# A two-layer decoder trunk: the order of Pool's adding transfers, and of three VectorE steps where the FFN begins

## What is computed

```python
for layer in range(DEPTH):                      # DEPTH = 2
    ...                                         # the mixing part: h = h + mix
    hn = rms_norm(h, norm_ffn_g[layer])
    h = h + (jax.nn.silu(hn @ ffn_w_gate[layer]) * (hn @ ffn_w_up[layer])) @ ffn_w_down[layer]
return rms_norm(h, norm_final_g)
```

## Time and profile before

| | |
|---|---|
| median of 3 runs | 561.09 us (559.78 to 562.26) |
| the profiled execution, its own time | 559.87 us |
| its span, first to last instruction | 558.0 us |
| granted PE clock | 0.999 of full speed, all through |
| PE busy | 548.7 us (98%) |
| DVE busy | 474.1 us (85%) |
| ACT busy | 348.9 us (63%) |

### The profile page before, as it was taken

The page is one execution under the profiler, slowest core; times in us unless marked ns, Lnnn a source line. Parts: engine busy times, 40 slices in busy tenths (PEclk is TensorE's granted clock), DMA queues, the critical chain, the costliest instruction groups (busy, mean ns, idle before and its releaser), DMA issues.

```text
span 558.0 us, 7380 instructions
## 1 busy us (share of the span) xinstructions
PE 548.7 (98%) x2805; PEld 461.0 (83%) x2805; DVE 474.1 (85%) x564; ACT 348.9 (63%) x475; POOL 29.0 (5%) x70
## 2 busy tenths in 40 slices
PE   8999999999999999999999999999999999999996
PEld 7899978887888788888888888888788888878785
DVE  5769996798989999878798998977989898989765
ACT  6877664664767486655666366646576666748524
POOL 1200001100000010000000000001010000000000
PEclk9999999999999999999999999999999999999999
DMA  8995546845979879774469422409789697977102
GB/s 295 409 404 196 189 150 211 270 123 132 298 258 286 307 203 340 189 286 167 151 256 346 174 76 76 151 29 292 284 221 339 187 314 243 295 284 211 56 0 75
DMA packets 32867, 122.42 MB, mean 219 GB/s; under 512 B 3648, under 2 KB 4800, under 8 KB 30784
## 3 DMA queue, kind: packets, MB, share of 16 engines
q1 hardware_dynamic: 30384, 105.04, 49.8%
q0 software_dynamic: 2304, 16.78, 15.7%
q10 hardware_dynamic: 144, 0.14, 0.1%
HBM read 120.89 MB, written 1.05 MB: 219 GB/s over the span
## 4 chain that ended last, share of the span: by engine, by line
PE 71%; DVE 16%; DMA 5%; issue 4%; ACT 3%; POOL 0%; SPq 0%; DVEq 0%; ACTq 0%; POOLq 0%
PE bank L1792 12%; PE bank L1794 12%; PE bank L1793 12%; DVE w_lo L1133 7%; PE bank L2266 5%; PE bank L2265 5%; PE bank L2270 5%; PE bank L1903 4%; PE bank L2237 3%; DMA spare<-in_slabs 2%; DMA sixth_raw<-in_slabs 2%; PE bank L1906 2%; DVE raw L1597 2%; PE bank L2242 1%; ACT w_hi L682 1%
## 5 line engine op out<-in xcount | busy, mean ns | idle before, releaser
L1133 DVE TENSOR_TENSOR w_lo<-raw,w_hi 128x2048 fp32r<-128x2048 f32 (+2 forms) x71 | 156.2, 2211 | 21.5 <-ACT w_hi L682 21.0
L682 ACT ACTIVATE w_hi<-raw 128x2048 fp32r<-128x2048 f32 (+2 forms) x66 | 120.8, 1846 | 5.0 <-DMA raw<-in_slabs 2.8
L1792 PE MATMUL bank<-w_lo,yT_hi 128*128 128x512 f32 (+1 forms) x226 | 91.3, 404 | 2.2 <-DVE yT_lo L1690 1.6
L1794 PE MATMUL bank<-w_hi,yT_lo 128*128 128x512 f32 (+1 forms) x226 | 88.1, 390 | 0.0
L1793 PE MATMUL bank<-w_hi,yT_hi 128*128 128x512 f32 (+1 forms) x226 | 87.8, 389 | 0.0
L1133 DVE TENSOR_TENSOR w_lo<-sixth_raw,w_hi 128x2048 fp32r<-128x2048 f32 x22 | 50.3, 2285 | 5.0 <-ACT w_hi L682 5.0
L1792 PEld LDWEIGHTS bank<-w_lo,yT_hi 128*128 128x128 f32 x226 | 42.5, 188 | 13.1 <-DVE yT_lo L1690 4.2
L2265 PE MATMUL bank<-w_hi,forms_hi 128*128 128x512 f32 x128 | 50.4, 394 | 0.0
L1794 PEld LDWEIGHTS bank<-w_hi,yT_lo 128*128 128x128 f32 x226 | 42.4, 188 | 9.1
L2266 PE MATMUL bank<-w_hi,forms_lo 128*128 128x512 f32 x128 | 49.9, 390 | 0.0
L1793 PEld LDWEIGHTS bank<-w_hi,yT_hi 128*128 128x128 f32 x226 | 42.6, 189 | 7.4
(11 more groups left out here) (289 smaller groups left out, 1136.5 us busy)
## 6 DMA issues: line engine op xcount, KB each, us to landing
raw<-in_slabs SPq DMA_DIRECT2D x146, 512.0 KB, 7.7
sixth_raw<-in_slabs SPq DMA_DIRECT2D x28, 512.0 KB, 7.6
sixth_raw<-in_slabs POOLq DMA_DIRECT2D x6, 1024.0 KB, 11.3
spare<-in_slabs SPq DMA_DIRECT2D x12, 512.0 KB, 4.9
raw<-in_slabs POOLq DMA_DIRECT2D x6, 1024.0 KB, 8.8
spare<-in_slabs POOLq DMA_DIRECT2D x4, 1024.0 KB, 10.4
raw<-in_slabs SPq DMA_DIRECT2D x5, 256.0 KB, 4.6
h<-in_x SPq DMA_DIRECT2D x2, 512.0 KB, 6.7
```

What stands on the lines that cost most here:

```text
L682: A(w_of(s, c), raw_of(r, c), ACT.Copy).then_inc(hi_ready, 1)
L1133: V.tensor_tensor(w_of(s, c, 1), raw_of(preps[s][0], c), w_of(s, c).bitcast(F32), ALU.subtract).then_inc(lo_ready, 1)
L1792: T.matmul(o, st_hi, mv_lo, start=first, stop=False, skip_group_check=onto)
L1794: return T.matmul(o, st_lo, mv_hi, start=False, stop=last, skip_group_check=onto)
```

## The change

There are two edits. First, Pool's order becomes T3(2), T4(2), T3(4), T3(6), T4(4), T3(8), T4(6), T4(8) in each layer. With two T3 possibly under way, `third_added` becomes two semaphores used in turn. Second, in the FFN's entry the gate `activate(3, 1)` and the low part `at_lo_evac(2, 0, 0, 1)` come ahead of the split of slab `f + 6`.

```diff
-        third_added = sem("third_added")
+        third_added = [sem(f"third_added{i}") for i in range(2)]
...
+        def third_sum(l, a):
+
+            n = seven_no(l, a)
+            return third_added[n % 2], 16 * (n // 2) + 16
+
         sum_of_prep = {}
...
-                sum_of_prep[place["t3", l, a]] = (third_added, 16 * seven_no(l, a) + 16)
+                sum_of_prep[place["t3", l, a]] = third_sum(l, a)
...
-                nc.gpsimd.dma_start(raw_of(y), piece(n, 0, SLAB), accum_op=ALU.add).then_inc(third_added, 16)
+                nc.gpsimd.dma_start(raw_of(y), piece(n, 0, SLAB), accum_op=ALU.add)\
+                    .then_inc(third_sum(l, a)[0], 16)
...
                 if (kind, a, b) in (("norm", 1, 1), ("norm", 3, 1)):
-                    for unit in SEVEN_AT[a // 2]:
-                        add_third(a // 2, unit)
-                        add_fourth(a // 2, unit)
+                    l, units = a // 2, SEVEN_AT[a // 2]
+                    add_third(l, units[0])
+                    add_fourth(l, units[0])
+                    add_third(l, units[1])
+                    for unit, following in zip(units[1:], units[2:]):
+                        add_third(l, following)
+                        add_fourth(l, unit)
+                    add_fourth(l, units[-1])
...
-                        dve.wait_ge(third_added, 16 * seven_no(l, a) + 16)
+                        dve.wait_ge(*third_sum(l, a))
...
                 block_add(SEVEN_AT[l][0], 0)
-                split_los(f + 6)
                 activate(3, 1)
                 at_lo_evac(2, 0, 0, 1)
+                split_los(f + 6)
                 split_forms()
```

## The result

| | before | after |
|---|---|---|
| median | 560.59 us (559.78 to 562.26) | 571.44 us (570.99 to 572.99) |
| ratio | | 1.0195, 95% interval 1.0163 to 1.0226 |
| profiled execution, own time | 559.87 us | 572.99 us |
| its span | 558.0 us | 571.2 us |

The change makes the kernel about 2% slower. The forecast was 571.0, and the time lies in its range of 562 to 577.

What follows compares the result with a forecast made beforehand. PE was taken as the bound, busy 548.7 of 558.0 us. 559.87 + 6.0 (layer 0) + 6.0 (layer 1) - 1.4 = 570.5; that execution lies 1.2 under the median, so 571, range 562 to 577.

Steps and rivals of the forecast that it cites:

- Pool's hold: Pool's queue: an adding transfer starts only 0.3 us after the one before has landed, so T4(4) waits for T3(6).
- The transfers: Unit 4's transfers to landing: T3(6) takes 9.0 us, T4(4) in the crowd 11.1, with bounds 7.8 twice and 12.6 twice.
- ACT's copy at landing + 4.2: ACT, unit 4: seven_copy(4, 2), needed by PE for b22, ends 4.2 us after T4(4) lands; layer 0 loss 5.7.
- DVE's way at landing + 14.0: DVE behind T4(4): PE's restart at 189.35 moves to landing plus 14.0, 195.4, 6.0 us later; the longer way.
- Layer 0: Unit 4 of layer 0: T4(4) lands at 181.4 instead of 174.6, costing +6.0 us, entry gain included.
- Layer 1: Unit 4 of layer 1: T4(4) lands at 456.4, the copy ends at 460.6 against b22 at 454.67, costing +6.0 us.
- The break in unit 8: Layer 1, block_add(8, 0): the wait for T3(8) goes, and with it PE's break at 495.89, -1.4 us.
- The entry: FFN entry: low part ready before PE needs it, worth 0.6 us in each layer unless lost at the next late thing.
- Quick transfers: Rival: T3(6) and T4(4) take 7.8 us each, sum 561.5, no change; chance 0.08.
- slow ones: Rival: T3(6) and T4(4) take 12.6 us each, +11.1 in each layer, sum 580.7; slow end beyond 577 has 0.06.
- Pool doesn't hold T4: Rival: T4(4) starts at 165.1 behind T3(6) and lands about as before; all four breaks go, 556.7 us; chance 0.08.
- the four breaks: PE's breaks in the FFNs, by the entry in both layers, at 189.35 and at 495.89: together 3.2 us, the most to gain.

Runs made afterwards that it cites:

- the run with 34 idle matmuls: Changed kernel with idle matmuls ahead of PE's wait at b22 of unit 4, 28 in layer 0 and 34 in layer 1: 571.33 us, ratio 1.0216.
- the run with twice the room: Changed kernel with descriptor room 1024 for 512 and five small buffers moved to make space: 562.38 us, ratio 1.0054.
- the aligned run: Changed kernel with room 1024, nmax and sums placed behind spare so forms_hi and forms_lo start at a multiple of 128 bytes: 561.17 us, ratio 1.0031.
- T4 first and room for both: Kernel before, with its Pool order kept, plus the entry edit and room 1024 with forms at a multiple of 128 bytes: 556.68 us, ratio 0.9950.

## Why the prediction was right, and where not

**Pool's hold.** Right: T4(4) starts 0.31 after T3(6) has landed, in both layers. That it is the same for a T4 behind a T3 was read from six T3 behind T4, and it held. The cause, which the prediction didn't have, is the descriptor room.

**The transfers.** T3(6) was put at 9.0 and took 7.9 and 8.1; T4(4) was put at 11.1 and took 12.7 and 10.8. The choice which of the two is quiet and which is in the crowd was right, and the sum of 20.1 stands against 20.6 and 18.9. In layer 0 the two errors offset each other (1.1 too high and 1.6 too low); in layer 1 both terms were too high. T4(4) of layer 0 went 0.1 past the upper bound of 12.6.

**The ways behind the landing.** ACT's copy at landing + 4.2 is exact (186.60, from 182.38). DVE's way at landing + 14.0 is nearly so: its low part ended at 196.52, which is 14.1. But the conclusion, that DVE's way is the longer one and sets +6.0, was wrong. PE reached the matmul that reads this low part only at 197.69, 1.2 after DVE was done:

```profile
196.10 0.42 DVE L1701 TENSOR_TENSOR yT_lo<-bank,yT_hi 128x256 fp32r<-128x256 f32 x1
...
197.69 0.39 PE L1803 MATMUL bank<-w_lo,yT_hi 128*128 128x512 f32 x1
```

The step that failed is that PE was taken to keep the pace of the earlier trace rows behind the break. At that pace PE would have come to this matmul 8.9 us behind b22, at 195.6, before DVE was done. With the clock at the lower level for 4 us, PE itself was the later one. The slow stretch costs 1.5 to 1.6 us in each layer between b22 and b11, as the run with 34 idle matmuls showed; 1.2 of it stands beyond DVE's way in layer 0.

**The terms.** Layer 0 was put at +6.0 and is +8.2: the landing is 1.0 later than forecast (182.4 for 181.4), and PE is another 1.2 behind DVE's way. Layer 1 was put at +6.0 and is +6.4, counted from the end of layer 0 (7.1 less the 0.7 that the entry gave). That it is so near is luck: counted in the same way the landing came 1.2 earlier than forecast (455.2 for 456.4) and b22 is +4.8, and the slow stretch, which was not in the sum, adds 1.6. The prediction also took ACT's way here and DVE's in layer 0, without a reason for the difference. The break in unit 8 was put at -1.4 and is -1.4. T4(6) was said not to be held, and is not. The sum of 570.5 for the profiled execution stands against 572.99 measured. So that 571 stands beside a median of 571.44 is in part luck, and closer than the terms are: the profiled execution was the slowest of its four, and the other three took 571.0 to 571.6.

**The entry.** Right in what it does (no break at 126, and none in layer 1) and in what it warned of, that it is lost again at the next late thing. In the changed kernel that is T4(4), in the kernel before the low parts behind a late T3. It wins about 1.5 once neither is late, which is near the 0.6 in each layer that the prediction put on it.

**The rivals.** Quick transfers (561.5) and slow ones (580.7) did not come. (The quick case lay outside the range of 562 to 577, though the prediction counted most of it in.) "Pool doesn't hold T4" was ruled out here, and the run with twice the room made its condition true: it gave 562.4, and 561.2 with the aligned layout, not 556.7. Its price took T4(4)'s landing as unchanged, and a transfer that moved beside another of its kind landed later (176.8 in the aligned run, 174.6 before). What it got right is the worth of the four breaks, 3.2: with T4 first and room for both they went, and the time was 556.68, 2.9 under the kernel before beside it. And the six T3 showed that Pool held a transfer with the room of 512; they did not show that it can't have two under way.

**Not settled.** Why 571.0 and 576.5 can both be times of the changed kernel stays open. The longest execution with a trace took 572.99; the one of 576.5 has none, and of it is known only that its granted clock was lower (0.979 over the whole, 0.987 to 0.988 in the other three of that set). How long T4(4) takes in the crowd was not controlled in any run.

## What to carry to other kernels

An idle time that the profile puts down to "issue" can have a holder that the profile doesn't name: look at what ended at that moment, and ask whether the new order hands the same hold to a transfer with less room behind it. Before reordering two transfers in one queue, ask why the second waits for the first; here it was room for descriptors, and more room won 0.5% (with the entry edit) where the new order lost 2%. And the breaks of 4.5 to 6.7 us in PE's stream had to be counted here together with the matmuls behind them, which ran at about half the pace until the clock rose.

## What the hardware showed that was not expected

- With a descriptor room of 512, Pool started an adding transfer of 1 MB 0.3 us after the one before had landed, never earlier, in all profiled runs with that room; with 1024 it was 0.55 us after the one before had started (164.21 and 164.76).
- Of two such transfers started 0.55 us apart (six pairs in each of the two runs with T4 first and the large room), the first took 8.0 to 10.1 us, where a T4 of the kernel before took 7.8 to 9.5, and the second 14.5 to 15.4. Started 3.1 to 3.3 us apart, the second took 11.2 to 12.4.
- After a standstill of 4.5 to 6.7 us (ten of them, in five runs), and in one run after one of 2.6, PE's granted clock was between 0.50 and 0.65 over the next 4.4 to 4.6 us, and while it was at the lower level 512-column matmuls started every 0.43 us. With idle matmuls in the standstill it stayed at 1.00.
- Products whose moving operand starts at a multiple of 128 bytes in its partition had a pitch of 226 to 227 ns; at an odd multiple of 64 it was 233 to 235, while products with `xT`, which stayed at a multiple of 128, kept 227 in the same run. The offsets are worked out from the sizes of the buffers; no row shows an address. One layout at an odd multiple of 64 was run, so that it is this offset and not another part of the layout is likely but not shown by itself.
